# A decoder layer in split fp32 on one core: the sample tokens' low columns read together with the high columns

## The reference, cut to what matters

```
x = x + 0.5 * SwiGLU_1(rmsnorm(x))            # D_MODEL 1024, D_FF 2816
h = rmsnorm(x); [u | q | k | v | q_mem] = h @ w_in        # 2048 columns
    pooling branch on u, block-sparse attention on q, k, v, cross-attention on q_mem
x = x + concat(A, B, C) @ w_out
x = x + 0.5 * SwiGLU_2(rmsnorm(x))

swiglu_ffn(x, g, w_in, w_out): gate, up = split(rmsnorm(x, g) @ w_in); return (silu(gate) * up) @ w_out
```

## Time and profile before

| | |
|---|---|
| time before, median of 3 runs | 561.38 us (560.51 to 562.12) |
| profiled execution | span 559.2 us from first to last instruction |
| between that span and the median | 2.2 us |
| PE busy | 551.3 us, 99% of the span |
| DVE busy | 398.9 us, 71% |
| ACT busy | 269.2 us, 48% |
| DMA | 128.40 MB, mean 230 GB/s |
| granted TensorE clock | 1.000 of full speed (mean of the span) |

### The profile page before, as it was taken

The page is one execution under the profiler, slowest core; times in us unless marked ns, Lnnn a source line. Parts: engine busy times, 40 slices in busy tenths (PEclk is TensorE's granted clock), DMA queues, the critical chain, the costliest instruction groups (busy, mean ns, idle before and its releaser), DMA issues.

```text
span 559.2 us, 13391 instructions
## 1 busy us (share of the span) xinstructions
PE 551.3 (99%) x5075; PEld 513.6 (92%) x5075; DVE 398.9 (71%) x715; ACT 269.2 (48%) x425; POOL 17.7 (3%) x24
## 2 busy tenths in 40 slices
PE   8999999999999999999999999999999999999997
PEld 8999999999899998666777679999999999999997
DVE  4687888885588877889946685689777777664444
ACT  5844464444543337344535785475444344433330
POOL 1000000000000003100000000140000000000000
PEclk9999999999999999999999999999999999999999
DMA  9799999784567664899999994566756666465523
GB/s 236 208 269 324 271 315 268 234 249 149 196 216 273 205 209 160 273 338 382 351 300 371 373 337 143 163 180 197 211 168 191 182 175 194 132 220 181 187 75 79
DMA packets 137481, 128.40 MB, mean 230 GB/s; under 512 B 10937, under 2 KB 108880, under 8 KB 137432
## 3 DMA queue, kind: packets, MB, share of 16 engines
q1 hardware_dynamic: 134703, 127.24, 72.8%
q10 hardware_dynamic: 2736, 0.61, 0.5%
HBM read 125.12 MB, written 2.83 MB: 229 GB/s over the span
## 4 chain that ended last, share of the span: by engine, by line
PE 85%; DVE 7%; DMA 3%; ACT 2%; issue 1%; SPq 0%; DVEq 0%; ACTq 0%
PE banks L1505 25%; PE banks L1506 25%; PE banks L1507 25%; PE banks L1665 3%; PE banks L1513 2%; DVE w_lo L1021 2%; PE banks L1939 1%; PE banks L1637 1%; DMA raw<-in_ffn_w_in 1%; PE banks L1890 1%; DMA x_rows<-in_x_sample 1%; DMA page_ids<-in_page_table 1%; PE banks L1866 1%; ACT x_hi L827 1%; DVE prob_pair L1448 1%
## 5 line engine op out<-in xcount | busy, mean ns | idle before, releaser
L701 ACT ACTIVATE w_hi<-raw 128x1024 fp32r<-128x1024 f32 x158 | 166.5, 1059 | 194.9 <-PE banks L1507 160.8
L1021 DVE TENSOR_TENSOR w_lo<-raw,w_hi 128x1024 fp32r<-128x1024 f32 x158 | 193.8, 1232 | 73.9 <-ACT w_hi L701 72.7
L1505 PE MATMUL banks<-x_hi,w_hi 128*128 128x264 f32 x752 | 214.1, 285 | 0.1
L1506 PE MATMUL banks<-x_lo,w_hi 128*128 128x264 f32 x752 | 213.0, 283 | 0.0
L1507 PE MATMUL banks<-x_hi,w_lo 128*128 128x264 f32 x752 | 213.0, 283 | 0.0
L1505 PEld LDWEIGHTS banks<-x_hi,w_hi 128*128 128x128 f32 x752 | 141.6, 188 | 0.7 <-issue 0.4
L1506 PEld LDWEIGHTS banks<-x_lo,w_hi 128*128 128x128 f32 x752 | 141.7, 188 | 0.0
L1507 PEld LDWEIGHTS banks<-x_hi,w_lo 128*128 128x128 f32 x752 | 141.0, 188 | 0.0
L1505 PE MATMUL banks<-h_hi,w_hi 128*128 (+1 forms) x352 | 100.2, 285 | 0.0
L1507 PE MATMUL banks<-h_hi,w_lo 128*128 (+1 forms) x352 | 100.2, 285 | 0.0
L1506 PE MATMUL banks<-h_lo,w_hi 128*128 (+1 forms) x352 | 100.0, 284 | 0.0
(11 more groups left out here) (287 smaller groups left out, 501.7 us busy)
## 6 DMA issues: line engine op xcount, KB each, us to landing
raw<-in_ffn_w_in SPq DMA_DIRECT2D x86, 512.0 KB, 4.8
raw<-in_ffn_w_out SPq DMA_DIRECT2D x44, 512.0 KB, 3.4
kv<-in_cache_k SPq DMA_DIRECT2D x56, 256.0 KB, 4.8
kv<-in_cache_v SPq DMA_DIRECT2D x48, 256.0 KB, 6.3
raw<-in_w_in SPq DMA_DIRECT2D x12, 512.0 KB, 5.2
late_slot<-in_cache_v SPq DMA_DIRECT2D x16, 256.0 KB, 4.6
raw<-in_w_out SPq DMA_DIRECT2D x8, 512.0 KB, 7.5
raw<-in_mem_w_kv SPq DMA_DIRECT2D x4, 512.0 KB, 4.0
```

What stands on the lines that cost most here:

```text
L701: act.activation(w_hi[:, n % RING, :], raw[:, n % RING, :], ACT.Copy).then_inc(hi_ready, 1)
L1021: vec.tensor_tensor(w_lo[:, n % RING, :], raw[:, n % RING, :], w_hi[:, n % RING, :].bitcast(F32), ALU.subtract).then_inc(lo_ready, 1)
L1505: pe.matmul(out, lhs[0], rhs[0], start=start, stop=False)
L1506: pe.matmul(out, lhs[0], rhs[1], start=False, stop=False)
```

## The change

There are `NW` = 272 columns in a new first matmul: the 264 high columns and, right behind them, the 8 low columns of the samples. For this x_hi and x_lo become two views of one tile `x_both`, and h_hi and h_lo one tile `h_both`, each [high 264 | low 264] per channel tile. The second matmul moves the 256 low columns of the prompt alone, and writes from column 8 on; the third is unchanged. The samples' low part thus lands in columns 264 to 271 of the bank, and has to be added to columns 0 to 7 by VectorE: in `gate` and in `up_hidden` with one more instruction each and a wait between, in `residual` with one more scalar_tensor_tensor per tile and a wait (`inst` 0 and 1), or with two for every four tiles (`inst` 2, where they also make xs, which ACT made before). rstd gets a copy of its first 8 columns at its end. The core of the diff:

```diff
+NW = N + NS
-        x_hi = place("x_hi", [P, KT, N], F32R)
-        x_lo = place("x_lo", [P, KT, N], F32R)
+        x_both = place("x_both", [P, KT, 2 * N], F32R)
+        x_hi, x_lo = x_both[:, :, 0:N], x_both[:, :, N:2 * N]
-        h_hi = place("h_hi", [P, HT, N], F32R)
-        h_lo = place("h_lo", [P, HT, N], F32R)
+        h_both = place("h_both", [P, HT * 2 * N], F32R)
...
+            def dense(out, lhs, rhs, start, stop):
+
+                pe.matmul(out[:, 0:NW], lhs[0], rhs(0, NW), start=start, stop=False)
+                pe.matmul(out[:, NS:N], lhs[0], rhs(NW, NP), start=False, stop=False)
+                return pe.matmul(out[:, 0:N], lhs[1], rhs(0, N), start=False, stop=stop)
...
+                    first = NS if g0 is None else 0
+                    if g0 is not None:
+                        vec.scalar_tensor_tensor(out=xT[:, m, 0:NS], in0=bank[m][:, N:NW], scalar=weight, in1=xT[:, m, 0:NS],
+                                                 op0=ALU.mult, op1=ALU.add).then_inc(res_samples, 1)
+                        vec.wait_ge(res_samples, KT * inst + idx + 1)
+                    vec.scalar_tensor_tensor(out=xT[:, m, first:N], in0=bank[m][:, first:N], scalar=weight, in1=xT[:, m, first:N],
                                              op0=ALU.mult, op1=ALU.add).then_inc(res_ready, 1)
...
+                    if g0 is None and idx % 4 == 3:
+                        some = M_ORDER[idx - 3]
+                        four = slice(some, some + 4)
+                        vec.scalar_tensor_tensor(out=xT[:, four, 0:NS], in0=banks[:, four, 0:NS], scalar=weight, in1=xT[:, four, 0:NS],
+                                                 op0=ALU.mult, op1=ALU.add).then_inc(res_samples, 1)
+                        vec.wait_ge(res_samples, KT * inst + idx // 4 + 1)
+                        vec.scalar_tensor_tensor(out=xs[:, four, :], in0=banks[:, four, N:NW], scalar=weight, in1=xT[:, four, 0:NS],
+                                                 op0=ALU.mult, op1=ALU.add).then_inc(xs_copied, 1)
...
-                vec.tensor_tensor(sg[:, s, :], bank[b0 + 2 * s][:, 0:N], rstd[:], ALU.mult).then_inc(gate_ready, 1)
+                vec.tensor_tensor(sg[:, s, :], bank[b0 + 2 * s][:, 0:NW], rstd[:], ALU.mult).then_inc(gate_scaled, 1)
+                vec.wait_ge(gate_scaled, c + (HT * f + 1))
+                vec.tensor_tensor(sg[:, s, 0:NS], sg[:, s, 0:NS], sg[:, s, N:NW], ALU.add).then_inc(gate_ready, 1)
...
+                vec.tensor_tensor(h_tmp[:, s, 0:NS], h_tmp[:, s, 0:NS], h_tmp[:, s, N:NW], ALU.add).then_inc(up_summed, 1)
+                vec.wait_ge(up_summed, c + (HT * f + 1))
```

More of the change, by code:

```diff
@@ L151, in layer @@
         root = place("root", [P, N])
-        rstd = place("rstd", [P, N])
+        rstd = place("rstd", [P, NW])
         rot = place("rot", [P, 4, 2, MH * HALF_ROT], at=cursor[0])
-        sg = place("sg", [P, 2, N])
+        sg = place("sg", [P, 2, NW])
         rows_m = place("rows_m", [P, NP], at=cursor[0])
@@ L1485, in _ @@
             vec.wait_ge(root_ready, 1)
-            vec.reciprocal(rstd[:], root[:]).then_inc(rstd_ready, 1)
-            vec.wait_ge(rstd_ready, 2)
+            vec.reciprocal(rstd[:, N:NW], root[:, 0:NS]).then_inc(rstd_ready, 1)
+            vec.reciprocal(rstd[:, 0:N], root[:]).then_inc(rstd_ready, 1)
+            vec.wait_ge(rstd_ready, 4)
             vec.wait_ge(mid_stored, 16 * MID_STORES)
@@ L1521, in ffn_unit @@
                         pe.wait_ge(xlo_ready, k_at + idx + 1)
-                    mm = three(bank[b0 + j][:, 0:N], weights(n % RING, k * P, (k + 1) * P),
-                               (x_hi[:, k, :], x_lo[:, k, :]), idx == 0, idx == KT - 1)
+                    mm = dense(bank[b0 + j], weights(n % RING, k * P, (k + 1) * P), tokens_of(k), idx == 0, idx == KT - 1)
                 mm.then_inc(w_used, 1)
@@ L1530, in ffn_unit_high_first @@
                 for idx, k in enumerate(M_ORDER):
-                    pe.matmul(bank[GU_BANK + j][:, 0:N], w_hi[:, n % RING, k * P:(k + 1) * P], x_hi[:, k, :], start=idx == 0, stop=False)
-                    pe.matmul(bank[GU_BANK + j][:, 0:N], w_hi[:, n % RING, k * P:(k + 1) * P], x_lo[:, k, :], start=False, stop=False)
+                    pe.matmul(bank[GU_BANK + j][:, 0:NW], w_hi[:, n % RING, k * P:(k + 1) * P], tokens_of(k)(0, NW), start=idx == 0, stop=False)
+                    pe.matmul(bank[GU_BANK + j][:, NS:N], w_hi[:, n % RING, k * P:(k + 1) * P], tokens_of(k)(NW, NP), start=False, stop=False)
                 pe.wait_ge(lo_ready, n + 1)
@@ L1565, in ffn_in_loop @@
                             ffn_unit(f, i, 2 * s + half)
-            hidden = lambda k: tuple(h[:, ds(k, 1), :].rearrange("p a n -> p (a n)") for h in (h_hi, h_lo))
+            hidden = lambda k: lambda c0, n: hidden_of(k, c0, n)
             def ffn_out(f):
@@ L1578, in ffn_out @@
                             pe.wait_ge(mkv_ready, 2)
-                        mm = three(bank[m][:, 0:N], weights((n0 + k) % RING, m * P, (m + 1) * P), hidden(k), k == 0, False)
+                        mm = dense(bank[m], weights((n0 + k) % RING, m * P, (m + 1) * P), hidden(k), k == 0, False)
                     mm.then_inc(w_used, 1)
@@ L1594, in outer @@
                 for m in order:
-                    mm = three(bank[m][:, 0:N], weights(n % RING, m * P, (m + 1) * P), x, False, False)
+                    mm = dense(bank[m], weights(n % RING, m * P, (m + 1) * P), x, False, False)
                 mm.then_inc(w_used, 1)
@@ L1734, in _ @@
                         pe.wait_ge(xlo_ready, k + 1)
-                        mm = three(bank[GU_BANK + j][:, 0:N], weights(j, k * P, (k + 1) * P), (x_hi[:, k, :], x_lo[:, k, :]),
-                                   k == 0, k == KT - 1)
+                        mm = dense(bank[GU_BANK + j], weights(j, k * P, (k + 1) * P), tokens_of(k), k == 0, k == KT - 1)
                     if half:
@@ L1765, in _ @@
             pe.wait_ge(c_loaded, 16 * 9)
-            mixed = [(x_hi[:, k, :], x_lo[:, k, :]) for k in MIX_K]
+            mixed = [tokens_of(k) for k in MIX_K]
             for what, k in steps():
@@ L1848, in _ @@
                         pe.wait_ge(pooled_ready, pr + 1)
-                        pe.matmul(bank[POOL_BANKS[pr]][:, 0:N], pool_wd[:, pr, :], sg[:, pr, :], start=True, stop=True).then_inc(pool_psum, 1)
+                        pe.matmul(bank[POOL_BANKS[pr]][:, 0:N], pool_wd[:, pr, :], sg[:, pr, 0:N], start=True, stop=True).then_inc(pool_psum, 1)
                 elif what == "HA":
```

41 lines of the change are left out of this document (22 added, 19 removed).

## The result

The changed kernel takes 567.13 us (median of 4 runs, 566.93 to 567.42), beside 561.57 us for the kernel before on the same chip: a ratio of 1.0101, with a 95% interval of 1.0087 to 1.0115. It is 5.6 us slower. The forecast was 563.9 us, 2.5 us slower: the right side, inside the stated range of 555.0 to 567.3, but above the 562.0 to 565.7 of the forecast's own case, and less than half of the loss.

A forecast was written before the change was run, and what follows sets the result against it. PE was taken to bound the kernel, busy 551.3 of 559.2 us. Terms 0 + 0.8 + 0.4 + 1.3 + 0 = 2.5 us gave a span of 561.7, plus 2.2 to the median: 563.9 us, range 555.0 to 567.3.

The forecast's parts named there:

- the forecast's own case: Whole kernel: widths and places cost nothing, VectorE's waits add 2.5 us, a third more or less; chance 0.55.
- Second residual: PE has nothing else to do while seven tiles' small instructions add 0.19 us each: +1.3 us.
- The samples' projection: After the first residual, xs is finished later than PE wanted it: +0.4 us with the handover.
- Unit 11: Start of FFN1: splits queue behind VectorE's longer hidden tiles 1 to 3 and PE waits: +0.8 us.
- The end of the kernel: Small instructions after tiles 3 and 7 lie beside waits or PE's last turns: 0, at most 0.3 us.
- The hiding in the steady stages: Steady FFN stages: VectorE grows from 73 to 80 us in 100, banks are double, PE waits for none.
- The price of widths: PE's triples: straight line, 0.427 ns per column and 8.5 ns fixed, triple stays 363.6 ns: 0 us.
- Steps of 16: Rival: a matmul pays for whole groups of 16 columns, 7.06 ns off a triple, 556.0 us; chance 0.22.
- coarser steps: Rival: coarser steps or a penalty 256 columns escape, down to 16.2 us off, 547.7 us; chance 0.08.
- binding weight load: Rival: 121.2 ns is one load's time, 256 columns save nothing, 272 cost more: +3.8 us, 567.7 us; chance 0.10.
- The rival in which the waits hide: Residuals' small instructions overlap more, only 1 us left, 562.4 us; no separate chance, within the forecast's 0.55.
- The new places in memory: PE's triples: a high tile every 528 columns put at nothing, within 1 ns a triple, 1.1 us either way.

The follow-up runs named there:

- e3_sums: Kernel before plus VectorE's sums and waits alone, in hidden tiles and the first two residuals, adding columns 8 to 15; 562.76 us, ratio 1.0035.
- e2_shape: Changed kernel without VectorE's sums and their waits, ScalarE making xs again; places and widths of the change kept; 562.78 us, ratio 1.0041.
- e1_place: Kernel before with only the new places: high and low parts side by side, still three matmuls of 264 columns; 562.52 us, ratio 1.0030.
- m1_rows: Kernel before plus, behind it, rows of single matmuls by width and place and rows of triples, into unread banks; 650.19 us in one run.
- e6_pool_waits: Changed kernel in which GpSimd waits, ahead of its third sum, until VectorE has normed the samples' queries and keys; 569.50 us, 1.0142 of kernel before.
- e9_x_pad: Changed kernel with eight unused columns ending each row of the input's two parts, so rows start at eight places; 567.01 us, ratio 1.0110.
- e4_h_side: Kernel before with only the hidden tiles' high and low parts side by side, the input's parts apart; 560.63 us, ratio 0.9983.
- e7_x_row272: Kernel before with the input's two separate tiles in rows of 272 columns, 264 used, so rows start at four places; 562.74 us, ratio 1.0020.

## Why the prediction was right or wrong

**VectorE's waits were right in place, but for the end, and near in size.** Second residual: 1.3 us forecast, 1.03 measured in the step (1.05 in e3_sums). The samples' projection: 0.4 forecast, 0.435 measured. Unit 11: 0.8 forecast, 0.44 measured against the kernel before; but the 400 ns of its profile is itself one draw from 121 to 527 in kernels without sums, against 829 to 1,583 with them, so that 0.4 to 1.2 is all that can be said. The period of a residual tile was to go from 0.75 to 0.94 us: it did, 0.744 to 0.944. VectorE's 80 us in 100: 80.8. The end of the kernel: 0 forecast, "at most 0.3 us", and 0.3 measured; the sum had it at nothing, because it let the path run through PE's last turns and not through VectorE's list, where the two small instructions stand ahead of the copies. e2_shape and e3_sums have the old end. e3_sums, with these waits alone, is 2.1 us slower by its medians and its span 2.5 us longer, against the 2.5 us of the sum. The hiding in the steady stages is right too.

**The price of widths was right.** It is a straight line, 0.44 ns a column where 0.427 was taken. 256, 264 and 272 measure 118.5, 120.3 and 126.2 ns at one place against the forecast's 117.8, 121.2 and 124.6, and the three steps in the changed kernel's first FFN add up to 2,920 / 8 = 365.0 ns a triple, where 363.6 was forecast; all of the excess over the 2,900 / 8 = 362.5 of before is there in e1_place as well. Steps of 16, coarser steps and a binding weight load all fall by m1_rows and e2_shape. The rival in which the waits hide falls by e3_sums.

**The step that failed** is a term of the sum: "The new places in memory (a high tile every 528 columns, not 264) I put at nothing, within 1 ns of a triple either way, 1.1 us." They cost 2.5 ns a triple in the first FFN and 4.2 in the second, 2.4 us in these stages (1.7 ns of the 4.2, 0.6 us, are the part that e6_pool_waits does not have with the same places). The bound of 1 ns had no row behind it: a trace with one layout can't show what another costs. The forecast gave "other losses, above all from places in memory" 0.05, and that was too little. It should have been an open term like the widths.

**What was missed** is the 0.73 us at the queries' turn. The prediction said that VectorE's rotation moves with the samples' projection, but not that GpSimd's sums beside it, fed by ScalarE's squares, move by another amount. The trace of before had the warning: of four instructions of one form, the shortest took 0.16 and the longest 0.75 us. That is 0.41 us; for the other 0.36, the late first rotation, no cause was found. e3_sums has such a pause, of 0.30 us, between its first and second rotation. Counted in the traces, it stands at the same place in VectorE's list in all four kernels with the sums: in front of the 425th recorded instruction, which is the first rotation in the changed kernel, e6_pool_waits and e9_x_pad and the second in e3_sums, which lacks an instruction ahead of it. So in these four the pause goes with the place in the list and not with what the instruction waits for. In e3_sums it costs PE nearly nothing, a turn of 428 ns. The Trainium skill has the rule (SBUF — State Buffer, Who interferes with whom): a VectorE instruction with two inputs in SBUF contends with a GpSimd instruction that reads SBUF, and the later one waits for the whole of the other. The traces agree: 0.56 to 0.75 us for those that end just behind a sum, 0.17 to 0.18 us for all six without one.

**The sum again,** in the span's 5.9 us: places 2.4, unit 11 0.4, samples' projection 0.4, the turn 0.7, second residual 1.1 (with 0.1 us in the step behind it), the end 0.3 make 5.3. Another 0.2 us are in the mix, whose 8 units read the input's tiles too: 0.17 us in the changed kernel, 0.11 to 0.18 in every kernel with these tiles moved, 0.00 in those with them as before, so this is places again. Some 0.3 us is in the attention over the memory, where the other kernels, which differ nowhere near, lie from 0.1 us below the kernel before to 0.6 above; 0.1 us is not attributed. The parts alone say the same: the spans of e2_shape (+2.4) and e3_sums (+2.5) make 4.9, and the turn and the end, which neither of them shows, bring it to 5.9. Each span is that of one execution, though, and such steps come and go between them (one of 0.95 us in e4_h_side).

**What stays open** is why a place costs what it does. Six layouts of the input gave 2,900 to 2,946 ns for one and the same work, the kernel before by a happy accident the best. One layout gave 2,920 in one stage and 2,934 in another, and in e7_x_row272 2,946 and 2,907, and the rows of matmuls alone did not predict the kernel's order of layouts.

## What to carry to other kernels

Where PE sets the time, a change of layout is a change of PE's price: 0.7 to 1.2% of a matmul here. Compare the starts of equal stretches over 20 units before and after, and give "the same columns elsewhere in memory" a term with a range, not a zero. A delay on one engine must also be followed to what then runs beside it: small VectorE instructions on the path cost three to nearly five times their price beside a GpSimd sum, and holding GpSimd back costs more if something waits for its sums.

## What the runs showed of the hardware that was not expected

- The start of a moving tile, over eight places 32 bytes apart, changes a matmul of 256 columns between 113.7 and 119.9 ns, and a triple of 264 between 360.0 and 370.2 ns, at one clock and with nothing else on PE. That the price repeats every 256 bytes was assumed, not tested. Moving only the low tile by 64 bytes cost 0.9% of every triple of the FFN's input stages (2,900 to 2,926 ns).
- Within a stage the step from unit to unit is the same to 1 ns over dozens of units (e9_x_pad's second FFN repeats 2,915, 2,939 and 2,906 ns instead), and the means over whole stages, 2,900, 2,906.7, 2,920, 2,926.6, 2,933.3 and 2,946.6 ns, lie 6.7 ns or a multiple of it apart. The same layout can settle on one of them in one stage and on another in the next.
- After a wait, VectorE's first instruction starts 0.10 us behind the copy that releases it in ten kernels and 0.46 us behind it in three, at one place in its list of instructions, for no reason that the traces show.
- The price of an fp32r matmul is linear from 240 to 512 columns, 0.44 ns a column (one per cycle at 2.4 GHz would be 0.417), with about 6 ns fixed (111.7 - 240 x 0.44).
- A VectorE instruction of 16 columns and 0.16 us with both inputs in SBUF lasts 0.51 to 0.76 us when it ends behind one of GpSimd's sums of about 0.75 us, and 0.17 us when GpSimd is held back.
